# Second attention in block products: another order of VectorE's, ScalarE's and TensorE's short steps, token sums made one head earlier

## The chip, the cores and the metric

One core of a Trainium2 chip runs the whole program. The metric is the device time of one execution in microseconds (us). Everything is float32; matmuls run on a high part and a low part of each operand (three passes: high x high, high x low, low x high), so every weight block is first copied to a rounded high part by ScalarE and the rest is made by VectorE.

## The reference, cut to what matters

Two transformer-like blocks run one after the other on 512 tokens of width 2048. The change lies in the second block's chunk attention:

```python
proj = h @ w_in[l]
a_q, a_k, a_v, a_z, g_q, g_f, g_i, g_z = jnp.split(proj, offsets, axis=-1)
...
q = _rms(q, q_g); k = _rms(k, k_g)
scores = einsum(q, kb) * (dh ** -0.5)
p = softmax(where(valid, scores + bias, -inf))
out = einsum(p, vb)
att = att * jax.nn.silu(a_z)
```

It has 8 heads of width 128. Then comes a gated recurrence (`hg`, 8 heads), and the output projection.

## The kernel before

TensorE works through phases. Phase `att` has 8 heads. Heads 0 and 1 are plain: four projections (query, key, value, gate), each of 16 steps of three 512-column matmuls. Heads 2 to 7 (`att_pairs`, L1239 for TensorE, L1906 for ScalarE, L2820 for VectorE) are made from *pairs*: the query and key tiles are one pair (`keys`), the value and gate tiles another (`values`). A pair is computed with seven block products instead of eight (a Strassen-like scheme): sums and differences of weight blocks and of token blocks are multiplied and the results combined. There are 12 pairs.

Names that the change touches:

- **Product n of pair q** (`pair_product`, L1206): 8 steps of three 256-column matmuls, 24 in all, into one PSUM bank. It waits for the low part of its weight block (`block_split`) and for its bank to have been read. `hooks` maps a step number to something that is put behind that step.
- **`pair_high(q, n)`** (ScalarE, L1767) copies a weight block of 128x1024 to its high part, **`pair_low(q, n)`** (VectorE, L2659) makes the low part. `SPLIT_AT` says in which place of the order block n comes: before it is 0, 1, 2, 6, 3, 4, 5.
- **`read_pair(q, n)`** (VectorE, L2673) reads a finished bank and combines it; `first_form` and `first_corner` (ScalarE) copy two corners.
- **Token blocks**: products of pair 0 need sums of token blocks of `Y`, made in place by `t_sums(0..3)` (VectorE, L2625), rounded by `t_high` (ScalarE) and completed by `t_low` (VectorE), in heads 0 to 2.
- **The head's tail.** After the four projections of head i the rest of that head runs while the products of head i+1 do: gate (`gate_softplus`, `gate_logged`, `gate_sigmoid`, `gate_silu`), the turned value (`turn_value`, then `value_highs`, `value_lo`), the turned probabilities (TensorE `turn_head`, ScalarE `probsT_att`, VectorE `probs_lows`; two PSUM banks are used in turn, so tile j waits for `probsT` and `probs_lows` of tile j-2), `weigh_head`, and `weighed`.
- **Norm and scores of head i** run in its own `values` pair: `pair_norm` / `square_lo` / TensorE `square_sum` / `pair_rows` / `pair_normed` for query (0) and key (1), then `high` and `low` of both, `first_keys`, then four `scores` and the softmax steps `soft_in`, `exps`, `soft_out`.
- **DMA.** SyncE reloads the blocks of the next pair when a block has been split (`next_pair`); GpSimd adds further blocks onto them in an accumulating DMA (`add_block`): into `raw_block(1, 0)` and into `block_sums` (shown as `mkv` in the trace).
- **The junction to `hg`** (`first_recurrence`, L1276): 48 matmuls of 512 columns, the first 24 on the token halves that were never overwritten, then 16 that need `act_hi` restored from memory and 8 that need `act_lo` restored (GpSimd, L3285). The tail of head 7 is hooked in. SyncE reloads seven heads of `Y` (1792 KB, L759) there.

The order on each engine is written out by hand. Each engine runs its own list in order and waits on semaphores, so a step that waits holds up what is behind it on its engine.

Of the kernel before, what the change touches and what calls it, by code (L numbers as in the profile page):

```python
# [157 lines left out]
def build(nc, wt, ada, bias, far_d, xT, memT, pw, cols_d, consts_d, starts_d, masks_d, spill, y_spill, block_spill, c_row,  # L158
          cum_rows, out):
    ctx = ExitStack()  # L160
    with ctx:
# [382 lines left out]
        SPLIT_AT = (1, 2, 3, 5, 6, 7, 4)  # L544
# [61 lines left out]
        def _(sp):  # L606
# [95 lines left out]
            def next_pair(q, between=None):  # L702

                sp.wait_ge(block_split.sem, block_split.at("pair", q, SPLIT_AT[1]))
# [5 lines left out]
                sp.wait_ge(block_split.sem, block_split.at("pair", q, SPLIT_AT[6]))  # L710
                sp.dma_start(raw_block(1, 1), pair_block(q + 1, 1, 1)).then_inc(s_block[3], 16)
                sp.wait_ge(block_split.sem, block_split.at("pair", q, SPLIT_AT[3]))
                sp.dma_start(raw_block(0, 1), pair_block(q + 1, 0, 1)).then_inc(s_block[1], 16)
                sp.wait_ge(block_split.sem, block_split.at("pair", q, SPLIT_AT[4]))
                sp.dma_start(block_sums[0], pair_block(q + 1, 0, 0)).then_inc(s_third, 16)
# [35 lines left out]
            for s, n in ((1, 6), (0, 3)):  # L751
                sp.wait_ge(block_split.sem, block_split.at("pair", NPAIR - 1, SPLIT_AT[n]))
                sp.dma_start(raw[:, slot("hg", s), :], wt[TILE0["hg"] + s]).then_inc(s_raw[slot("hg", s)], 16)
# [3 lines left out]
            sp.wait_ge(product_done.sem, product_done.at("pair", NPAIR - 1, 5))  # L757
            sp.wait_ge(s_att, 16 * (NATT - 1))
            sp.dma_start(Y[:, 0:NATT - 1, :], y_spill.rearrange("k p s -> p k s")).then_inc(s_reload, 16)  # L759
            loop(sp, "hg", lambda i: [load("hg", i, j) for j in range(4)])  # L760
# [59 lines left out]
        def _(pe):  # L820
# [385 lines left out]
            def pair_product(q, n, hooks=None):  # L1206

                i, v = q // 2 + NPLAIN, q % 2
                pe.wait_ge(block_split.sem, block_split.at("pair", q, SPLIT_AT[n]))
# [29 lines left out]
            def att_pairs(i):  # L1239
# [8 lines left out]

                pair_product(keys, 0)
# [3 lines left out]
                if i > NPLAIN:  # L1253
                    turn_head(i - 1, (0, 1))
                pair_product(keys, 2)
                if i > NPLAIN:
# [3 lines left out]
                if i > NPLAIN:  # L1260
                    weigh_head(i - 1)
# [3 lines left out]
                pair_product(values, 1, {2: lambda: square_sum(1)})  # L1265
                pair_product(values, 2, {2: lambda: score(0), 6: lambda: score(1)})
# [9 lines left out]
            def first_recurrence():  # L1276
# [15 lines left out]
                hooks = {0: lambda: turn_value("att", head, 2, qkv2[:, 2, :], QT), 5: lambda: turn_head(head, (0, 1)),  # L1292
# [142 lines left out]
        def _(act):  # L1435
# [353 lines left out]
            def att(i):  # L1789
# [65 lines left out]
                gate_exp("att", i, 3, dst=2)  # L1855
                if i == NPLAIN - 1:
                    pair_high(0, 2)
# [48 lines left out]
            def att_pairs(i):  # L1906
                keys, values = pair_no(i, 0), pair_no(i, 1)
                tail = i > NPLAIN
                pair_high(keys, 6)
                if tail:  # L1910
                    gate_softplus(i - 1)
                else:
                    t_high(1)
                first_form(keys)
                if tail:
                    value_highs(i - 1)
                else:
                    t_high(3)
                pair_high(keys, 3)
                if tail:  # L1920
                    gate_sigmoid(i - 1)
                    probsT_att(i - 1, 0)
                    probsT_att(i - 1, 1)
                pair_high(keys, 4)
                if tail:
                    probsT_att(i - 1, 2)
                    probsT_att(i - 1, 3)
                first_corner(keys)
                pair_high(keys, 5)
# [7 lines left out]
                high("att", i, 0, qk2_hi, qkv2)  # L1937
                pair_rows(i, 1)
                first_form(values)
                pair_high(values, 3)  # L1940
                high("att", i, 1, qk2_hi, qkv2)
                pair_high(values, 4)
                for t in range(2):
                    exps("att", i, t, tp2[:, 0, :])
                first_corner(values)
                pair_high(values, 5)
# [148 lines left out]
        def _(dve):  # L2095
# [563 lines left out]
            def pair_low(q, n):  # L2659

                dve.wait_ge(block_hi.sem, block_hi.at("pair", q, SPLIT_AT[n]))
# [3 lines left out]
            def pair_sum(q):  # L2665
# [3 lines left out]
                if q:  # L2669
                    dve.wait_ge(block_split.sem, block_split.at("pair", q - 1, SPLIT_AT[5]))  # L2670
# [41 lines left out]
            def att(i):  # L2712
# [30 lines left out]
                else:  # L2743
                    split("att", i, 0)
                    t_sums(0)
                    t_sums(1)
                    square_lo("att", i, 0, sq2_hi[:, :], sq2_lo[:, :])
# [6 lines left out]
                else:  # L2754
                    t_sums(2)
# [18 lines left out]
                if i == NPLAIN - 1:  # L2774
                    t_sums(3)
# [3 lines left out]
                if i == NPLAIN - 1:  # L2779
                    pair_sum(0)  # L2780
                    pair_low(0, 0)
                    pair_low(0, 1)
                if i:
                    dve.wait_ge(s_att, 16 * i)
                silu_gate("att", i, 3, wk[:, 2, :])
                weighed(i)
                if i == NPLAIN - 1:
                    t_low(2)
                    pair_low(0, 2)
# [30 lines left out]
            def att_pairs(i):  # L2820
# [6 lines left out]
                pair_low(keys, 6)  # L2827
                if tail:
                    gate_logged(i - 1)
                    value_lo("att", i - 1, v2_lo, v2_hi)  # L2830
# [607 lines left out]
```

## Time and profile before

| | us |
|---|---|
| Median of 3 runs (1877.53 to 1880.18) | 1877.79 |
| The profiled execution, its own time | 1876.38 |
| Its span, first to last instruction | 1874.6 |
| TensorE busy, of the span | 1847.6 |
| VectorE busy | 1381.3 |
| ScalarE busy | 875.4 |
| GpSimd busy | 243.4 |
| Mean granted TensorE clock | 0.995 of full |

TensorE is busy 99% of the span, but its matmuls overlap in the record (a 256-column matmul is recorded as 0.28 us and the next starts 0.12 us later), so busy time hides where the issue rate halves. Waits that are recorded as idle, and distances between starts, say more. Head h of the pair stage starts at 983.73, 1034.32, 1085.90, 1137.56, 1189.15 and 1239.24 us for h = 2 to 7.

### The profile page before, as it was taken

What the parts mean: (1) busy time and instruction counts of PE and PEld (TensorE: products, weight loads), DVE (VectorE), ACT (ScalarE), POOL (GpSimd) and SP (SyncE); (2) the same over time, 40 slices, a digit from 0 to 9 for tenths busy, and PEclk for the clock granted to TensorE, in tenths of its full rate; (3) what the DMA queues carried; (4) which work ended last, traced back from release to release, by engine and by line L of the source; (5) the groups of instructions that cost most, each with busy time, mean ns of one, the idle gap of its engine ahead of it and who ended that gap; (6) DMA issues with size and microseconds to landing.
All of it is one profiled execution on the core that took longest, in us unless ns stands there. A gap on an engine that the chain in (4) does not pass through costs nothing.

```text
span 1874.6 us, 28099 instructions
## 1 busy us (share of the span) xinstructions
PE 1847.6 (99%) x10006; PEld 1590.4 (85%) x10006; DVE 1381.3 (74%) x2011; ACT 875.4 (47%) x1310; POOL 243.4 (13%) x241
## 2 busy tenths in 40 slices
PE   9999999999999999999998999999999999999999
PEld 8888888888888877887888999998888888888999
DVE  6765678888888877777777677776666666659986
ACT  6543433333333373224545555554555555556333
POOL 3500000000000003442001011000122221111121
PEclk9999999999999999999999999999999999999999
DMA  7344244554445426675337666666222222123442
GB/s 282 112 158 180 70 163 171 179 178 164 161 168 177 148 101 232 231 252 184 116 110 182 181 165 162 170 173 197 68 90 90 70 86 90 67 90 124 147 157 91
DMA packets 68620, 278.25 MB, mean 148 GB/s; under 512 B 7352, under 2 KB 12984, under 8 KB 52288
## 3 DMA queue, kind: packets, MB, share of 16 engines
q1 hardware_dynamic: 60832, 253.08, 39.0%
q0 software_dynamic: 7264, 20.97, 6.2%
q10 hardware_dynamic: 448, 3.17, 0.4%
q8 instruction: 49, 0.80, 0.2%
q14 instruction: 27, 0.22, 0.0%
HBM read 264.85 MB, written 12.35 MB: 148 GB/s over the span
## 4 chain that ended last, share of the span: by engine, by line
PE 83%; DVE 9%; ACT 4%; issue 3%; DMA 1%; DVEq 0%; POOL 0%; ACTq 0%; another core or an unknown queue 0%; POOLq 0%
PE ps_p L843 20%; PE ps_p L845 20%; PE ps_p L844 20%; DVE w_lo L2662 2%; ACT w_hi L1771 1%; PE ps_o L1008 1%; PE ps_s L1323 1%; PE ps_t L1425 1%; PE ps_p L1231 1%; PE ps_p L1232 1%; PE ps_p L1233 1%; PE ps_t L1426 1%; PE ps_t L1424 1%; PE ps_s L1425 1%; PE ps_s L1424 1%
## 5 line engine op out<-in xcount | busy, mean ns | idle before, releaser
L843 PE MATMUL ps_p<-act_hi,w_hi 128*128 128x512 f32 x1680 | 672.6, 400 | 0.3 <-DVE w_lo L2116 0.3
L845 PE MATMUL ps_p<-act_hi,w_lo 128*128 128x512 f32 x1680 | 655.9, 390 | 0.0
L844 PE MATMUL ps_p<-act_lo,w_hi 128*128 128x512 f32 x1680 | 654.6, 390 | 0.0
L845 PEld LDWEIGHTS ps_p<-act_hi,w_lo 128*128 128x128 f32 x1680 | 315.3, 188 | 68.7
L843 PEld LDWEIGHTS ps_p<-act_hi,w_hi 128*128 128x128 f32 x1680 | 315.8, 188 | 60.6 <-issue 1.2
L844 PEld LDWEIGHTS ps_p<-act_lo,w_hi 128*128 128x128 f32 x1680 | 316.2, 188 | 59.6 <-issue 0.7
L1448 ACT ACTIVATE w_hi<-raw 128x2048 fp32r<-128x2048 f32 x117 | 223.7, 1912 | 268.3 <-PE ps_p L845 251.3
L2111 DVE TENSOR_TENSOR w_lo<-raw,w_hi 128x2048 fp32r<-128x2048 f32 x115 | 263.8, 2294 | 59.5 <-ACT w_hi L1448 48.2
L2406 DVE CUSTOM_DVE_ANT_0 mkv<-mkv,c_all 128x1024 f32<-128x1024 f32 x96 | 145.7, 1554 | 3.7 <-DVE wk L2153 2.9
L3261 POOL TENSOR_TENSOR ssq_a<-ssq_a,wk 128x512 f32<-128x512 f32 x15 | 36.3, 2420 | 724.6 <-ACT wk L1712 724.6
L1232 PE MATMUL ps_p<-y_lows,w_hi 128*128 128x256 f32 x384 | 109.4, 285 | 0.0
L1608 ACT ACTIVATE tp<-tp,stat 128x128 f32<-128x128 f32 (+1 forms) x64 | 36.1, 564 | 141.7 <-DVE stat L2375 141.7
L2245 DVE SCALAR_TENSOR_TENSOR Y<-upad,cols,Y 128x512 f32<-128x512 f32 x120 | 82.1, 747 | 0.0
L3301 POOL TENSOR_TENSOR hz<-hqk,hd 128x128 f32<-128x128 f32 x48 | 34.0, 707 | 327.0 <-DVEq L2985 288.2
L1232 PEld LDWEIGHTS ps_p<-y_lows,w_hi 128*128 128x128 f32 x384 | 73.7, 192 | 0.3
L2662 DVE TENSOR_TENSOR w_lo<-mkv,w_hi 128x1024 fp32r<-128x1024 f32 x36 | 44.0, 1223 | 36.5 <-ACT w_hi L1771 36.5
L2662 DVE TENSOR_TENSOR w_lo<-raw,w_hi 128x1024 fp32r<-128x1024 f32 x48 | 58.6, 1222 | 9.3 <-ACT w_hi L1771 9.2
L1231 PE MATMUL ps_p<-act_hi,w_hi 128*128 128x256 f32 x192 | 54.8, 285 | 1.9 <-DVE qkv L2681 1.9
L2076 ACT ACTIVATE w_hi<-mkv 128x1024 fp32r<-128x1024 f32 x24 | 25.5, 1061 | 62.2 <-DVE mkv L3125 32.9
L1233 PE MATMUL ps_p<-act_hi,w_lo 128*128 128x256 f32 x192 | 54.3, 283 | 0.0
L3268 POOL DMA_DIRECT2D mkv<-wt_dram x24 | 21.0, 877 | 253.3 <-DMA mkv<-wt_dram 128.5
L1771 ACT ACTIVATE w_hi<-raw 128x1024 fp32r<-128x1024 f32 x48 | 50.3, 1050 | 6.0 <-PE ps_p L1233 6.0
(520 smaller groups left out, 3599.8 us busy)
## 6 DMA issues: line engine op xcount, KB each, us to landing
raw<-wt_dram SPq DMA_DIRECT2D x122, 1024.0 KB, 4.9
mkv<-ada_dram SPq DMA_DIRECT2D x96, 512.0 KB, 4.6
raw<-wt_dram SPq DMA_DIRECT2D x68, 512.0 KB, 5.1
mkv<-wt_dram POOLq DMA_DIRECT2D x24, 512.0 KB, 5.9
mkv<-wt_dram SPq DMA_DIRECT2D x12, 512.0 KB, 6.3
raw<-wt_dram POOLq DMA_DIRECT2D x12, 512.0 KB, 8.8
qkv<-xT_dram SPq DMA_DIRECT2D x16, 256.0 KB, 2.8
spill_dram<-Y SPq DMA_DIRECT2D x16, 256.0 KB, 2.4
```

Of the source, the lines that this page charges most:

```text
L843: mm(o, wh, hi[:, k, 0:n], start=at == 0, stop=False)
L844: mm(o, wh, lo[:, k, 0:n], start=False, stop=False)
L845: last = mm(o, wl, hi[:, k, 0:n], start=False, stop=at == KT - 1)
L1231: mm(o, wh[:, c], hi, start=n < 3 and k == 0, stop=False, skip_group_check=True)
L1232: mm(o, wh[:, c], lo, start=False, stop=False, skip_group_check=True)
L1233: last = mm(o, wl[:, c], hi, start=False, stop=k == HALF_K - 1, skip_group_check=True)
L1448: fn(w_hi[:, s, :], raw[:, s, :], ACT.Copy).then_inc(w_hi_done, 1)
L1771: fn(fast_slot(n, w_hi), PAIR_FROM[n], ACT.Copy).then_inc(block_hi.sem, 1)
L2111: tt(w_lo[:, s, :], raw[:, s, :], w_hi[:, s, :].bitcast(F32), ALU.subtract).then_inc(w_split, 1)
L2245: o.step(stt(Y[:, c, :], upad[:, c, bass.ds(tap, S)], cols[:, bass.ds(tap + (w0 + c * TAPS), 1)], Y[:, c, :], ALU.mult, ALU.add))
L2406: dve.tensor_tensor_reduce(out=w, in0=w, in1=c_all[:, n % 2 * ADA_PIECE:(n % 2 + 1) * ADA_PIECE], scale=1.0, scalar=0.0, op0=ALU.mult, op1 ...
L2662: tt(fast_slot(n, w_lo), PAIR_FROM[n], fast_slot(n, w_hi).bitcast(F32), ALU.subtract).then_inc(block_split.sem, 1)
```

## The change

- The low and high parts of a pair's weight blocks are made in the order 0 to 6; `SPLIT_AT` is gone. Block 6 moves from the fourth place to the last. SyncE's reloads follow that order, so `raw_block(1, 1)` is reloaded last and not third.
- TensorE: transposes 2 and 3 of a head's probabilities move from between products 2 and 3 into product 3 (behind its steps 1 and 4). The second square sum goes one step later, the first score from step 2 to step 4 of product 2, the second score from step 6 to behind that product.
- ScalarE and VectorE: `probs_lows` 0 and 1 are made together; the key's norm comes ahead of the query's `pair_rows`; `high` and `low` of query and key come together; blocks 3, 5 and 6 of the `values` pair take other places.
- Head 0 takes `t_sums(0)`, head 1 takes `t_sums(1)` to `(3)` a place earlier and `t_low(2)` too; in head 1's gate the steps are mixed with `pair_high(0, 2)` and `pair_low(0, 2)`.
- Junction to `hg`: the split of the first tile comes behind the fourth `soft_in`, the head-7 weighing ahead of the wait for `act_lo`, the value's transposes two steps later. The two first tiles are loaded in the other order, and the reload of `Y` waits for two more tile loads.

```diff
-        SPLIT_AT = (1, 2, 3, 5, 6, 7, 4)
 next_pair (SyncE), behind raw_block(1, 0) and raw_block(0, 0):
-                sp.wait_ge(block_split.sem, block_split.at("pair", q, SPLIT_AT[6]))
+                sp.wait_ge(block_split.sem, block_split.at("pair", q, 4))
+                sp.dma_start(raw_block(0, 1), pair_block(q + 1, 0, 1)).then_inc(s_block[1], 16)
+                sp.wait_ge(block_split.sem, block_split.at("pair", q, 5))
+                sp.dma_start(block_sums[0], pair_block(q + 1, 0, 0)).then_inc(s_third, 16)
+                sp.wait_ge(block_split.sem, block_split.at("pair", q, 7))
                 sp.dma_start(raw_block(1, 1), pair_block(q + 1, 1, 1)).then_inc(s_block[3], 16)
-                (raw_block(0, 1) behind SPLIT_AT[3], block_sums[0] behind SPLIT_AT[4])
 SyncE, junction:
-            for s, n in ((1, 6), (0, 3)):
+            for s, n in ((0, 3), (1, 6)):
+            def hg(i):
+                for j in range(4):
+                    load("hg", i, j)
+                    if isinstance(i, int) and j == 1:
+                        (the reload of Y, which stood ahead of the loop)
 TensorE, att_pairs:
                 pair_product(keys, 2)
-                if i > NPLAIN:
-                    turn_head(i - 1, (2, 3))
-                pair_product(keys, 3)
+                pair_product(keys, 3, {1: turn(2), 4: turn(3)} if tail else None)
...
-                pair_product(values, 1, {2: lambda: square_sum(1)})
-                pair_product(values, 2, {2: lambda: score(0), 6: lambda: score(1)})
+                pair_product(values, 1, {3: lambda: square_sum(1)})
+                pair_product(values, 2, {4: lambda: score(0)})
+                score(1)
 TensorE, first_recurrence:
-                hooks = {0: lambda: turn_value(...), 5: ..., 7: ...}
+                hooks = {2: lambda: turn_value(...), 5: ..., 7: ...}
...
+                weigh_head(head)
                 pe.wait_ge(s_add[1], RESTORED)
                 for k in range(HALF_K):
                     ins = step(k, lambda wh, wl, hi, lo: ((wh, lo),), last=k == HALF_K - 1)
-                    if k == 4:
-                        weigh_head(head)
 ScalarE, att_pairs:
-                pair_high(keys, 6)
...
                 pair_high(keys, 5)
-                for n in range(2):
-                    pair_high(values, n)
+                first_corner(keys)
+                pair_high(keys, 6)
+                pair_high(values, 0)
+                pair_high(values, 1)
                 pair_norm(i, 0)
                 pair_high(values, 2)
+                pair_norm(i, 1)
                 pair_rows(i, 0)
-                pair_norm(i, 1)
-                pair_high(values, 6)
+                pair_high(values, 3)
+                pair_rows(i, 1)
+                high(query), high(key), first_form(values), pair_high(values, 4), exps 0,
+                pair_high(values, 5), exps 1, first_corner(values), pair_high(values, 6), exps 2
 VectorE, att_pairs:
-                pair_low(keys, 6)
...
                 read_pair(keys, 0)
                 if tail:
                     probs_lows(i - 1, 0)
+                    probs_lows(i - 1, 1)
                 pair_low(keys, 4)
-                    probs_lows(i - 1, 1)
                 read_pair(keys, 1)
...
                 pair_low(keys, 5)
+                pair_low(keys, 6)
...
+                square_lo("att", i, 1, sq2_hi[:, :], sq2_lo[:, :])
                 pair_normed(i, 0)
-                square_lo("att", i, 1, sq2_hi[:, :], sq2_lo[:, :])
-                pair_low(values, 6)
-                low("att", i, 0, qk2_lo, qkv2, qk2_hi)
+                pair_low(values, 3)
                 pair_normed(i, 1)
                 first_keys(i)
-                pair_low(values, 3)
-                read_pair(values, 0)
+                low("att", i, 0, qk2_lo, qkv2, qk2_hi)
                 low("att", i, 1, qk2_lo, qkv2, qk2_hi)
                 o.settle()
                 dve.sem_inc(qk_ready.sem, 1)
+                read_pair(values, 0)
...
                 soft_in("att", i, 2, lambda t, e: add_bias(i, t, e))
+                pair_low(values, 6)
...
-                else:
-                    split("hg", 0, -1)
                 soft_in("att", i, 3, lambda t, e: add_bias(i, t, e))
                 bias_read(i)
+                if i == NATT - 1:
+                    split("hg", 0, -1)
 VectorE, att (heads 0 and 1): t_sums(0) goes to the end of head 0, t_sums(1), (2), (3)
 one place earlier, t_low(2) ahead of value_lo; pair_low(0, 2) between the gate's two steps.
```

## Rows read from the trace of the kernel before

**Rows 1.** Page part 1, TensorE and the others over the whole span

```profile
PE 1847.6 (99%) x10006; PEld 1590.4 (85%) x10006; DVE 1381.3 (74%) x2011; ACT 875.4 (47%) x1310; POOL 243.4 (13%) x241
```

**Rows 2.** Waits of TensorE, 960 to 1320: total us, times, longest

```profile
PE ps_t L992 <- DVE p_lo L2709: 8.2, 10, 1.5
PE ps_x L959 <- DVE sq_lo L2694: 4.0, 6, 0.7
PE ps_s L980 <- DVEq L2867: 2.8, 6, 0.5
PE ps_p L1231 <- DVE w_lo L2662: 2.0, 1, 2.0
PE ps_p L1231 <- DVE qkv L2681: 1.9, 1, 1.9
PE ps_p L1284 <- DVE qkv L2687: 1.8, 1, 1.8
PE ps_p L1284 <- DMA act_lo<-block_spill_dram: 0.5, 1, 0.5
```

**Rows 3.** Windows of heads 2, 4, 6: length, busy, granted clock, DMA share

```profile
983.73:1034.32 50.59, 45.59 (x351) 44.46 (x352) 39.98 (x56) 28.19 (x42) 5.16 (x6) 0.97 0.69 172
1085.90:1137.56 51.66, 48.88 (x379) 47.48 (x377) 36.74 (x62) 27.79 (x47) 5.18 (x6) 0.97 0.67 171
1187.40:1237.50 50.10, 47.31 (x378) 46.01 (x378) 36.75 (x63) 27.78 (x46) 5.19 (x6) 1.00 0.68 176
```

**Rows 4.** Timeline of TensorE, head 4: start, duration, line, idle before

```profile
1092.12 0.93 PE L992 MATMUL ps_t<-consts,tp 128*128 128x128 f32 x7
1092.81 0.36 PE L1231 MATMUL ps_p<-th_mid,w_hi 128*128 128x256 f32 x1
...
1098.16 0.36 PE L1231 MATMUL ps_s<-act_hi,w_hi 128*128 128x256 f32 x1
...
1102.60 0.28 PE L1231 MATMUL ps_p<-act_hi,w_hi 128*128 128x256 f32 x1
...
1105.47 0.69 PE L1008 MATMUL ps_o<-tp_r,v_hi 128*128 128x512 f32 x3
...
1107.20 0.36 PE L1231 MATMUL ps_p<-act_hi,w_hi 128*128 128x256 f32 x1
...
1116.37 0.28 PE L1231 MATMUL ps_p<-th_short,w_hi 128*128 128x256 f32 x1
...
1118.27 0.47 PE L959 MATMUL ps_x<-sq_hi,ones_r 128*128 128x512 f32 x1 [0.67 <-DVE sq_lo L2694]
```

**Rows 5.** Timelines of VectorE and ScalarE, heads 2 and 4

```profile
988.23 2.28 DVE L2657 TENSOR_TENSOR y_lows<-Y,th_mid 128x2048 fp32r<-128x2048 f32 x1
...
1095.27 0.68 DVE L2709 TENSOR_TENSOR p_lo<-ps_t,tp_r 128x512 fp32r<-128x512 f32 x1
1096.12 1.23 DVE L2662 TENSOR_TENSOR w_lo<-mkv,w_hi 128x1024 fp32r<-128x1024 f32 x1 [0.17 <-ACT w_hi L1771]
...
1114.78 0.69 ACT L1901 ACTIVATE wk<-ps_x,cols 128x512 f32<-128x512 f32 x1 [1.72 <-PE ps_x L960]
...
1116.12 0.62 ACT L1892 ACTIVATE wk<-qkv 128x512 f32<-128x512 f32 x1
```

**Rows 6.** Timeline of TensorE at the junction to hg

```profile
1290.72 0.28 PE L1233 MATMUL ps_p<-act_lo,w_lo 128*128 128x256 f32 x1
...
1309.86 0.40 PE L843 MATMUL ps_p<-act_hi,w_hi 128*128 128x512 f32 x1
...
1310.55 0.40 PE L843 MATMUL ps_p<-act_hi,w_hi 128*128 128x512 f32 x1
```

**Rows 7.** DMA issues at the junction (1285 to 1292) and at 1089.87: KB, us to landing

```profile
act_hi<-block_spill_dram POOLq DMA_DIRECT2D x1, 1024.0 KB, 6.0
act_lo<-block_spill_dram POOLq DMA_DIRECT2D x1, 1024.0 KB, 14.8
...
mkv<-wt_dram POOLq DMA_DIRECT2D x1, 512.0 KB, 7.9
```

More of the change, by code:

```diff
@@ L756, in _ @@
             load("hg", 0, -1)
[L757 to L760, printed above, removed]
+            def hg(i):
+                for j in range(4):
+                    load("hg", i, j)
+                    if isinstance(i, int) and j == 1:
+                        sp.wait_ge(product_done.sem, product_done.at("pair", NPAIR - 1, 5))
+                        sp.wait_ge(s_att, 16 * (NATT - 1))
+                        sp.dma_start(Y[:, 0:NATT - 1, :], y_spill.rearrange("k p s -> p k s")).then_inc(s_reload, 16)
+            loop(sp, "hg", hg, head=1)
             for j in range(2):
@@ L1854, in att @@
                         pair_high(0, n)
-                gate_exp("att", i, 3, dst=2)
-                if i == NPLAIN - 1:
-                    pair_high(0, 2)
+                if i < NPLAIN - 1:
+                    gate_exp("att", i, 3, dst=2)
+                    return
+                act.wait_ge(proj_done, tile_no("att", i, 3) + 2)
+                act.wait_ge(heads_done.sem, heads_done.at("att", i, 0))
+                softplus(wk[:, 2, :], ps_p[:, slot("att", 3), :]).then_inc(gate_soft.sem, 1)
+                pair_high(0, 2)
+                gate_sigmoid(i)
             def value_highs(i):
@@ L1927, in att_pairs @@
                     probsT_att(i - 1, 3)
+                pair_high(keys, 5)
                 first_corner(keys)
-                pair_high(keys, 5)
-                for n in range(2):
-                    pair_high(values, n)
+                pair_high(keys, 6)
+                pair_high(values, 0)
+                pair_high(values, 1)
                 pair_norm(i, 0)
                 pair_high(values, 2)
+                pair_norm(i, 1)
                 pair_rows(i, 0)
-                pair_norm(i, 1)
-                pair_high(values, 6)
[L1937 to L1946, printed above, removed]
+                pair_high(values, 3)
+                pair_rows(i, 1)
+                high("att", i, 0, qk2_hi, qkv2)
+                high("att", i, 1, qk2_hi, qkv2)
+                first_form(values)
+                pair_high(values, 4)
+                exps("att", i, 0, tp2[:, 0, :])
+                pair_high(values, 5)
+                exps("att", i, 1, tp2[:, 0, :])
+                first_corner(values)
+                pair_high(values, 6)
                 exps("att", i, 2, tp2[:, 0, :])
@@ L2774, in att @@
                 if i == NPLAIN - 1:
-                    t_sums(3)
+                    t_low(2)
                 value_lo("att", i, v2_lo, v2_hi)
@@ L2782, in att @@
                     pair_low(0, 1)
+                else:
+                    t_sums(0)
                 if i:
                     dve.wait_ge(s_att, 16 * i)
-                silu_gate("att", i, 3, wk[:, 2, :])
+                log_sigmoid("att", i, 3, 1, wk[:, 2, :])
+                if i == NPLAIN - 1:
+                    pair_low(0, 2)
+                do(tt(wk[:, 3, :], ps_p[:, slot("att", 3), :], wk[:, 2, :], ALU.mult))
+                dve.sem_inc(evac[slot("att", 3)], 1)
                 weighed(i)
-                if i == NPLAIN - 1:
-                    t_low(2)
-                    pair_low(0, 2)
             def bias_read(i):
@@ L2830, in att_pairs @@
                     value_lo("att", i - 1, v2_lo, v2_hi)
+                else:
+                    t_low(1)
                 pair_low(keys, 3)
-                if not tail:
-                    t_low(1)
                 read_pair(keys, 0)
@@ L2836, in att_pairs @@
                     probs_lows(i - 1, 0)
+                    probs_lows(i - 1, 1)
                 pair_low(keys, 4)
-                if not tail:
-                    t_low(3)
-                if tail:
-                    probs_lows(i - 1, 1)
                 read_pair(keys, 1)
```

43 lines of the change are left out of this document (22 added, 21 removed).

## The prediction

> **What bounds the kernel now.** I read the page's first part, then TensorE's waits, then windows over single heads, then the timeline of TensorE across one head, and last the timelines of the two engines that feed it. TensorE is busy 99% of the span [rows 1], so nothing outside its own path can matter much, and nothing that only shortens VectorE or ScalarE. But the busy share hides two things. The waits of the pair stage and of the junction add up to 8.2 + 4.0 + 2.8 + 2.0 + 1.9 + 1.8 + 0.5 = 21.2 us [rows 2]: nearly all of TensorE's idle time in the whole kernel (1874.6 - 1847.6 = 27) stands in the 330 us that the diff touches. And the windows show something that is in no wait: head 4 takes 51.66 at a granted clock of 0.97, head 6 takes 50.10 at 1.00, with the same work [rows 3]. Five of the six heads (2, 3, 4, 5 and 7) have it.
>
> The timeline says where. A product is 24 matmuls and takes 1105.47 - 1102.60 = 2.87 at the full clock [rows 4]. Seven transposes take 1092.81 - 1092.12 = 0.69, so 0.1 each, and the weighing of a head 1107.20 - 1105.47 = 1.73 [rows 4]. Product 2 of `keys` and the three transposes behind it start at 1092.81 and product 3 at 1098.16: 5.35 where 2.87 + 0.3 = 3.17 is work, so 2.18 lost. Product 3 then takes 1102.60 - 1098.16 = 4.44 instead of 2.87: 1.57 lost, because after that gap the granted clock fell to its lower level (1.2 instead of 2.4 GHz) for a stretch. The difference of the heads' windows, 51.66 - 50.10 = 1.56, is that same 1.57 [rows 3]: the gap stood in head 6 as well and the clock didn't fall there. After the shorter waits (0.7 and 0.5) no fall shows.
>
> **The change part by part.**
>
> *Transposes 2 and 3.* What they wait for is a chain: the tail's softplus, the value, the sigmoid and `probsT` 0 on ScalarE, then `probs_lows` 0 on VectorE, 1095.27 to 1095.95; then `pair_low(keys, 4)`, which itself waits 0.17, 1096.12 to 1097.35; then `probs_lows` 1, which the last transpose needs [rows 5]. Nothing in the diff makes the first link earlier: the block-6 pieces that go away ran in time in which VectorE waited for the softplus and ScalarE for a read bank. So `probs_lows` 0 is ready at 1095.95 as now, plus about 0.15 to reach TensorE. TensorE asks for it later: product 3 can start at 1092.81 + 2.87 = 1095.7, two steps (6 matmuls of 0.12) end at 1096.4. That is 0.3 of slack where 2.18 were lost. `probs_lows` 1 now follows at once: done by 1095.95 + 0.68 = 1096.6 at most, and asked for after three more steps and transpose 2, at 1096.4 + 0.2 + 1.08 = 1097.7: 1.0 of slack. Behind them, `pair_low(keys, 4)` ends near 1097.8 and is asked for by product 4 at 1095.7 + 2.87 + 0.3 = 1098.9. So the whole loss goes: 2.18 for each of heads 3 to 7 and 1.57 for four of them, 10.9 + 6.3 = 17.2. The bounds: if transpose 2 were 0.5 late each time and the clock fell as now, 2.5 + 6.3 would stay, and 8 be gained; nothing can be gained beyond 17.2.
>
> *Second square sum.* From 1116.37 to 1118.27 stand nine matmuls (1.08): 0.82 lost a head [rows 4]. ScalarE ran `pair_rows(0)` from 1114.78 ahead of the key's norm at 1116.12, 1.34 [rows 5]. Now the norm is first, so its low part comes 1.3 earlier, and TensorE asks 0.36 later. 0.82 x 6 = 4.9 gained. The price is that `pair_rows(0)` comes 1.3 later, and with it the first score, which has moved by two steps (0.7) and whose path loses `pair_low(values, 6)` (1.22, a piece as in [rows 5]); I count that as slack of about 0.5.
>
> *Second score.* 2.8 in six heads [rows 2], with a restart of 0.1 each 0.55 a head. Its path loses `pair_low(values, 6)` and `read_pair(values, 0)`, 1.6 together, and it is asked for after the product instead of one step before its end. 3.3 gained.
>
> *Head 2 (first pairs).* TensorE waits 2.0 for block 2's low part and 1.9 for `read_pair(0, 1)` [rows 2], and the clock is 0.97 over the 50.59 [rows 3], so another 1.5 as in head 4. In front of both stands `t_low(2)`, 2.28 at 988.23 [rows 5], between the weighing of head 1 and `pair_low(0, 2)`. It now runs in head 1 where `t_sums(3)` ran, and `t_sums(0)` runs at the end of head 0, where VectorE waits for the gate's softplus anyway. `pair_low(0, 2)` comes out of the gate's own waits at about 987.5, and product 2 asks at 983.73 + 2 x 2.9 = 989.6. `t_low(1)` then ends at 991.1 and block 3 at 992.3, which product 3 wants at 992.5: the tightest spot, 0.1. `t_low(3)` and block 5 end at 997.9 before 998.3. Gain 2.0 + 1.9 + 1.5 = 5.4, between 3 and 6.
>
> *The block-6 pieces* are moved into idle stretches of both engines (VectorE is busy 37 of 51.7 [rows 3]) with nothing waiting behind them but the softmax steps. *The reloads*: block (1, 1) is issued some 10 us later in the pair and needed last. What is needed earlier than before is the accumulated `block_sums[1]`: `pair_high(keys, 5)` used to wait for a free slot until late and will now start right behind `probsT` 3, about 12.3 after the head's start. Its DMA is issued 1089.87 - 1085.90 = 4.0 after the start and lands 7.9 later [rows 7], at 11.9. So 0.4 of slack on ScalarE, and 2.8 more until product 5 asks. I cost it at nothing.
>
> *Junction.* From the end of the last product (1290.72 + 0.12) to the next projection (1309.86) are 19.0 [rows 6]. Work in it: 48 matmuls of (1310.55 - 1309.86) / 3 = 0.23, so 11.0, and 1.73 for weighing and 14 transposes of 0.1: 14.2 [rows 4, 6]. The loss of 4.8 is the 1.8 wait for `read_pair(values, 3)`, the 0.5 wait for the restored `act_lo` [rows 2], and a stretch at the lower clock. With block 5 earlier in the last pair VectorE reaches the split of the first `hg` tile and then `read_pair(values, 3)` before the last product ends; the wait goes, and the low clock after it. TensorE then arrives some 4 us sooner at `act_lo`, which landed only at 1291.31 + 14.8 = 1306.1 [rows 7]. That DMA ran beside 1792 KB of `Y`; its twin of the same size and form took 6.0 alone. With `Y` behind two more tile loads I take 8 (between 6.0 and 14.8, nearer to the undisturbed row), so 1299.4, and the weighing now stands ahead of that wait: no wait. If it kept its 14.8, TensorE would be held to 1306.1 + 8 x 0.23 = 1307.9, and 1.9 would be the whole gain of the junction. Against the gain: `hg`'s second tile is now loaded as its block 6 is split, 6.5 before the last product's end, beside the restore of `act_hi`, and the last tail's chain starts behind its split. I take 4.0 gained, between 0 and 4.8.
>
> On such transfers the Trainium skill (DMA: Bandwidth & Descriptors, "Issuing engines are not separate DMA queues") has a rule that speaks against this part: DMAs started by sync, scalar or gpsimd interleave on the same 16 engines. By that rule the second tile and `act_hi`, issued by two engines at one time, slow each other, and the last tail starts later; the sum would then be some 2 us worse. The same rule is what makes moving `Y` worth something. The trace agrees, with 14.8 against 6.0 for one form [rows 7].
>
> **Sum.** 17.2 + 4.9 + 3.3 + 5.4 + 4.0 = 34.8. Each tight spot has 0.1 to 0.5 of slack worked out from rows that agree within 0.1, so a few tenths will stay here and there; I take off 1.5. Against the profiled execution: 1876.4 - 33.3 = 1843.1. The median of the runs lies 1.4 above it: 1877.8 - 33.3 = 1844.5. I say 1844.
>
> **The rivals.**
>
> *A: the short waits stay in part.* The 0.3 at transpose 2 and the 0.5 at the first score may be negative by as much. Each then costs its lateness, and if the clock falls, 1.57 a head as now. For: the softplus chain is untouched by the change. Against: gaps of 0.7 and 0.5 did not bring the clock down in any of six heads. Price: about 10 to 14 back, of which 6.3 clock: 1855 to 1858.
>
> *B: the junction gives nothing* (`act_lo` as late as now or the last tail late behind the tile). 4.0 back: 1848. It lies in the forecast's own range.
>
> *C: slower, by the accumulating DMA.* `pair_high(keys, 5)` now stands on ScalarE ahead of the corner, block 6, both first blocks of `values` and the norm, so a late `block_sums[1]` holds them all. It has 0.4 + 2.8 of slack and 5.2 of gain a head to eat: the change turns slower from a landing of 7.9 + 3.2 + 5.2 = 16.3 on. The row shows 7.9, and even twice the size beside `Y` took 14.8 [rows 7]. At 18 it costs 10 us more than now: 1887.
>
> *D: nothing*: the waits are put down to the wrong releaser and others stand right behind each. For: three engines run in near lockstep here. Against: the chain above leaves slack at every one. About 1876.
>
> **How the numbers follow.** Forecast (with B in it, 1839 to 1850) 0.74; A 0.16; something between A and D 0.05; D 0.02; C 0.03. The range 1838 to 1857 holds the forecast and most of A. A measurement of this kernel can tell about 0.2% (3.8 us) from no change. Faster by more: 0.95; within: 0.02; slower: 0.03.
>
> **What would show it.** After: heads 3 to 7 of about 46.5 us each with granted clock 1.00, head 2 of about 44 to 45; no wait of L992 over 0.3; L959 and L980 waits near zero; the wait for `read_pair(0, 1)` and block 2 gone; junction of 14.5 to 16; `act_lo` landing in under 10. Heads at 48 or more with a clock of 0.97 mean A. A wait of ScalarE's L1771 for `mkv`'s DMA means C. The plain heads and `hg`, `out2` and `fast` should keep their lengths; if `hg` head 0 grows, the later reload of `Y` is in the way of its tiles, which I have taken to have 20 us of room.

## The result and the profile after

| | us |
|---|---|
| Median before, in the runs beside those of after | 1877.71 (1877.53 to 1880.18) |
| Median after, 4 runs | 1844.88 (1843.74 to 1845.87) |
| Ratio, 95% interval | 0.9822 (0.9805 to 0.9839) |
| Profiled execution after, its own time / its span | 1844.08 / 1842.2 |

The profiled execution is 32.3 us shorter (1876.38 - 1844.08); predicted were 33.3. The places it came from, by the starts of the heads in both timelines (head 2 starts at 983.46 after):

| | before | after | gained | predicted |
|---|---|---|---|---|
| head 2 | 50.59 | 47.91 | 2.7 | 6.8 (5.4, and 0.82 + 0.55) |
| heads 3 to 7 | 256.5 | 231.1 | 25.4 | 24.05 (17.2, and 5 x 1.37) |
| junction | 19.0 | 14.96 | 4.1 | 4.0 |

The page's first part, which answers [rows 1]:

```profile
PE 1833.5 (100%) x10006; PEld 1582.1 (86%) x10006; DVE 1380.2 (75%) x2011; ACT 875.7 (48%) x1310; POOL 243.5 (13%) x241
```

VectorE and ScalarE do as much as before; only TensorE's record shrank, by 14 us, less than half of the gain. The waits of TensorE from 960 to 1320 (total us, times, longest) answer [rows 2]:

```profile
PE ps_t L1235 <- DVE w_lo L2673: 2.3, 1, 2.3
PE ps_s L1235 <- DVE w_lo L2673: 0.3, 1, 0.3
PE ps_x L963 <- DVE sq_lo L2705: 0.2, 1, 0.2
PE ps_t L996 <- DVE p_lo L2720: 0.2, 1, 0.2
```

Of 21.2 us 3.0 are left, and the largest, 2.3, is a wait that was not there before. The windows of heads 2, 4 and 6 and of the junction (length, busy, granted clock, DMA share, GB/s) answer [rows 3]:

```profile
983.46:1031.37 47.91, 45.18 (x352) 44.08 (x352) 37.50 (x55) 28.49 (x42) 5.16 (x6) 0.96 0.72 182
1077.59:1123.84 46.25, 46.25 (x378) 45.81 (x377) 36.57 (x62) 27.78 (x47) 5.18 (x6) 1.00 0.77 192
1170.05:1216.30 46.25, 46.25 (x378) 45.81 (x377) 36.56 (x62) 27.77 (x47) 5.18 (x6) 1.00 0.77 191
1262.51:1277.47 14.96, 14.74 (x75) 12.00 (x74) 8.29 (x13) 6.47 (x11) 0.89 (x1) 1.00 0.90 250
```

Heads 4 and 6 have no idle time and the full clock, and are now equally long; before, they differed by 1.56. (The window that [rows 3] gives for head 6 begins 1.75 before the head; by its own starts, 1189.15 to 1239.24, the head takes 50.09, so the reading stands.) TensorE's timeline of head 4 (start, duration, line) answers [rows 4]: the first row of product 3, its two hooked transposes, and the later places of the second square sum and of the scores:

```profile
1087.38 0.28 PE L1235 MATMUL ps_s<-act_hi,w_hi 128*128 128x256 f32 x1
...
1088.11 0.38 PE L996 MATMUL ps_t<-consts,tp 128*128 128x128 f32 x2
...
1089.40 0.27 PE L996 MATMUL ps_t<-consts,tp 128*128 128x128 f32 x1
...
1105.80 0.39 PE L963 MATMUL ps_x<-sq_hi,ones_r 128*128 128x512 f32 x1
...
1109.47 0.38 PE L979 MATMUL ps_s<-tp,qkv 128*128 128x128 f32 x2
1110.76 0.28 PE L984 MATMUL ps_s<-qk_hi 128*128 128x256 f32 x1
```

None has an idle note. Head 2 is the exception. Its timelines on SyncE, GpSimd, ScalarE, VectorE and TensorE, in the order of the chain:

```profile
989.20 0.33 SPq L695 DMA_DIRECT2D y_spill_dram<-wk  x1
989.63 0.42 SPq L705 DMA_DIRECT2D raw<-wt_dram  x1
...
997.49 0.86 POOL L3281 DMA_DIRECT2D raw<-wt_dram  x1 [8.60 <-DMA raw<-wt_dram]
...
1004.13 1.06 ACT L1777 ACTIVATE w_hi<-raw 128x1024 fp32r<-128x1024 f32 x1 [4.57 <-DMA raw<-wt_dram]
...
1004.19 1.23 DVE L2682 TENSOR_TENSOR mkv<-raw 128x1024 f32<-128x1024 f32 x1 [5.08 <-issue]
1005.33 1.22 DVE L2673 TENSOR_TENSOR w_lo<-raw,w_hi 128x1024 fp32r<-128x1024 f32 x1
...
1006.61 0.57 PE L1235 MATMUL ps_t<-act_hi,w_hi 128*128 128x256 f32 x1 [2.27 <-DVE w_lo L2673]
1006.97 0.42 PE L1236 MATMUL ps_t<-act_lo,w_hi 128*128 128x256 f32 x1
```

SyncE's store of head 1 (L695) stands ahead of the load of `raw_block(1, 0)` (L705) and waits for the weighing. The load is issued at 989.63 and lands 7.6 later; GpSimd adds onto it (lands 6.6 later, at 1004.1); only then can ScalarE round it and VectorE make `pair_sum(values)` and the low part. Matmuls behind the wait start 0.21 apart and not 0.12: the granted clock from 1006.60 to 1009.10 is 0.51. Before, the same chain was ready about as late: its load, issued behind the store at 988.77, landed 4.6 later, and GpSimd's addition landed 9.8 after its issue, at 1003.5 (GpSimd's row in the timeline, and the row of the DMA issues with KB and us to landing):

```profile
993.68 0.86 POOL L3268 DMA_DIRECT2D raw<-wt_dram  x1 [0.88 <-DMA raw<-wt_dram]
```

```profile
raw<-wt_dram POOLq DMA_DIRECT2D x1, 512.0 KB, 9.8
```

But TensorE, held up by its two earlier waits, came only at 1009.8.

### The profile page after: what moved, and what is told of

It reads as the page before. It is cut to its first block, busy times and chain, and to the rows that moved or that the text cites. A ratio compares the mean times of both kernels' runs of the same rounds, so it can differ in the third digit from the quotient of the medians.

```text
span 1842.2 us, 28086 instructions
## 1 busy us (share of the span) xinstructions
PE 1833.5 (100%) x10006; PEld 1582.1 (86%) x10006; DVE 1380.2 (75%) x2011; ACT 875.7 (48%) x1310; POOL 243.5 (13%) x241
## 4 chain that ended last, share of the span: by engine, by line
PE 93%; DVE 5%; issue 1%; ACT 1%; DMA 0%; DVEq 0%; SPq 0%; another core or an unknown queue 0%; ACTq 0%
PE ps_p L847 20%; PE ps_p L849 20%; PE ps_p L848 20%; PE ps_p L1236 3%; PE ps_p L1237 3%; PE ps_p L1235 3%; PE ps_o L1012 1%; PE ps_s L1329 1%; PE ps_t L1431 1%; PE ps_t L1432 1%; PE ps_t L1430 1%; PE ps_t L996 1%; PE ps_s L1431 1%; PE ps_s L1430 1%; PE ps_s L1432 1%
## 5 line engine op out<-in xcount | busy, mean ns | idle before, releaser
L3274 POOL TENSOR_TENSOR ssq_a<-ssq_a,wk 128x512 f32<-128x512 f32 x15 | 36.3, 2420 | 724.7 <-ACT wk L1718 724.7
```

## The experiments

Twelve kernels. *Period* is the distance from one weighing to the next, mean over heads 3 to 6 (the kernel after: 46.23; the kernel before: 51.23, mean of head starts 1034.32 to 1239.24). The medians of before beside them were 1876.6 to 1877.7. The runs were spread over four chips, but all profiles start this stage together (the weighing ahead of head 2 stands between 981.30 and 981.76).

**e1_turns_back**, on the kernel after:

```diff
-                pair_product(keys, 3, {1: turn(2), 4: turn(3)} if tail else None)
+                if tail:
+                    turn_head(i - 1, (2, 3))
+                pair_product(keys, 3)
```

> The changed kernel with one part undone: TensorE makes transposes 2 and 3 of the head before between products 2 and 3 again, in heads 3 to 7; VectorE and ScalarE keep their new order. Theory 1 (the loss follows the size of the wait): VectorE now rounds the two probability blocks one after the other right behind product 2's eviction, so TensorE waits about 1 us a head where it waited 2.18, and stays at full clock: 5 heads x 1 = 5 us, 1850. Rival (any stop at this place halves the clock behind it): the 1.57 us of half clock comes with it in each head: 5 x 2.6 = 13 us, 1858. Rival A of the prediction (the order on VectorE was the cause, the place on TensorE is idle talk): nothing, 1845.

Measured 1847.63 (1846.28 to 1848.71). Period 46.50: 0.27 a head, 1.35 in all, and no wait is recorded at these transposes; they take 0.51 between the products. The rest stands in head 2, which this edit does not touch: there this profiled run has a wait of 3.74 where after has 2.27, a second one of 1.11 at the square sum where after has 0.20, and a stretch at the lower clock (matmuls 0.21 apart from 1011.4 to 1015.9). By its median the run lies midway between theory 1 and the third reading; by the period the third is nearest: with VectorE's new order the place on TensorE hardly matters.

**e2_hooks_only**, on the kernel before:

```diff
-                if i > NPLAIN:
-                    turn_head(i - 1, (2, 3))
-                pair_product(keys, 3)
+                pair_product(keys, 3, {1: lambda: turn_head(i - 1, (2,)), 4: lambda: turn_head(i - 1, (3,))}
+                             if i > NPLAIN else None)
```

> The kernel before with one part of the change alone: TensorE makes transposes 2 and 3 inside product 3 (after its second and fifth step) in heads 3 to 7; VectorE and ScalarE keep the old order. Theory: product 3's matmuls cover the evictions that the transposes waited for, so nearly all of 17.2 us goes: 1877.8 - 15 to 17 = 1861 to 1863. Rival (the hooks come too early for VectorE's old order, which rounds probability block 3 only behind the next low block): the wait moves into product 3, at most half goes: 1868 or more.

Measured 1863.95 (1862.56 to 1864.64), 13.7 below before. Period 48.28, 2.95 below before, with the granted clock at 1.00 from 1051.8 to 1245. Waits of TensorE, 960 to 1320:

```profile
PE ps_x L959 <- DVE sq_lo L2693: 4.0, 6, 0.7
PE ps_p L1283 <- DMA act_lo<-block_spill_dram: 3.0, 1, 3.0
PE ps_s L980 <- DVEq L2866: 3.0, 6, 0.6
```

The ten waits at the transposes are gone, with VectorE's old order; the heads gain what the theory says. Heads 3 to 7 take 241.3, 15.2 less than before. Two places gave some of it back: the wait for `act_lo` grew from 0.5 to 3.0, which made the junction 20.1 long, 1.1 more than before, and head 2 took 1.4 more, where the clock fell twice and not once. So in heads 3 to 7 the same edit is worth 15 where it is the first and 1.4 where it is the last.

**e3_norm_back**, on the kernel after: `pair_rows(0)` ahead of the key's norm on ScalarE, `pair_normed(0)` ahead of the second square on VectorE.

```diff
-                pair_norm(i, 1)
                 pair_rows(i, 0)
+                pair_norm(i, 1)
```

> The changed kernel with the order of the second attention's norm step undone: VectorE normalises pair 0 ahead of the second square, ScalarE makes its rows ahead of the second norm. Theory (the term of the prediction holds): TensorE's second square sum waits 0.8 us again and the second score 0.55 us again in some or all heads: 1.37 x 6 = 8 us if both return, 4.9 if only the first, so 1850 to 1853. Rival (the waits had been produced by the late start of the step, which the other parts have also changed): 1845 to 1846.

Measured 1848.81 (1847.34 to 1849.99). Period 46.77: 0.54 a head, of which 0.31 is recorded as a wait (L963), and the score does not wait. The wait in head 2 was 3.65 in this run. In between the two theories: about 3.2 for six heads, not 4.9; the rest of the 3.9 between the medians goes with the longer wait in head 2.

**e5_store_later**, on the kernel after, in head 2 only:

```diff
-                    if i == NPLAIN:
-                        store_head(i - 1)
-                    next_pair(pair_no(i, 0))
+                    next_pair(pair_no(i, 0), between=(lambda: store_head(i - 1)) if i == NPLAIN else None)
```

> The changed kernel with one edit more: in head 2, SyncE issues the two raw block loads of its first pair ahead of the store of head 1, not behind it. The store waits for the weighing at 989.17 us of the profiled run, so the loads wait with it and are issued at 989.63; ahead of it they could go at about 984.6. Theory (the wait of 2.27 us ahead of the first values product of head 2 comes from this chain: load 7.6 us, POOL's accumulating transfer 6.6 us, ScalarE's high part, VectorE's pair sum): the wait goes, and with it the half clock behind it; head 2 falls from 47.9 to some 44 to 45 us and the kernel to 1841. Rival (the keys product's evictions, or VectorE's own queue, are as late anyway): the wait goes down by under 0.5 us, the time stays at 1844.5 or more.

Measured 1839.56 (1839.53 to 1839.66), 5.3 below after, ratio to before 0.9795 (0.9782 to 0.9809). SyncE, GpSimd and ScalarE in head 2:

```profile
984.45 0.33 SPq L705 DMA_DIRECT2D raw<-wt_dram  x1
...
988.84 0.86 POOL L3279 DMA_DIRECT2D raw<-wt_dram  x1
...
998.55 1.06 ACT L1775 ACTIVATE w_hi<-raw 128x1024 fp32r<-128x1024 f32 x1 [0.66 <-PE ps_p L1235]
```

The load goes 5.2 earlier and the wait is gone; the weighings of heads 1 and 2 are 61.41 apart, 65.79 after: 4.4 gained, so head 2 takes 43.5, 7.1 below before where 6.8 were predicted. The chain is shown, by the trace and by the medians, though the intervals of the two ratios to before just touch (0.9809 here, 0.9805 for after). This is also the fastest kernel of the study. Its five runs lie within 0.13 us, those of after within 2.1: so most of that spread came with this chain. All further runs start from this kernel, as differences of 0.3 us can be seen on it.

**f1_lows_back**:

```diff
 VectorE:
                     probs_lows(i - 1, 0)
-                    probs_lows(i - 1, 1)
                 pair_low(keys, 4)
+                if tail:
+                    probs_lows(i - 1, 1)
```

> Base of this and the next runs: the changed kernel with the two raw loads ahead of the store (1839.6 us, five runs within 0.13). Here one part is undone: VectorE rounds probability block 3 (the second probs_lows) behind pair_low(keys, 4) again; TensorE's two transposes stay inside product 3. Theory (two edits that each cover the same wait: the product in front hides what VectorE is late by): TensorE loses some 0.3 us a head, as it lost 0.27 a head when only the transposes went back: 1841. Rival (VectorE's order carries the gain, TensorE's place only the rest): 1.5 us or more a head, 1847.

Measured 1839.70 (1839.55 to 1839.81), period 46.23: nothing. **f2_both_back** has this edit and that of e1:

> The same base with both parts undone: VectorE's old place for probability block 3 and TensorE's old place for transposes 2 and 3. Theory (either alone would do, so the gain of 17.2 us in the prediction belongs to both together): the loss is far above the sum of the two single ones (0.3 + 0.3 a head): 2.2 of wait a head, 11 us, and 1.6 more in the heads where the granted clock falls behind it: 1851 to 1857. Rival (the rest of VectorE's new order has already moved these blocks): the sum of the two, 1842 to 1843.

Measured 1848.14 (1847.98 to 1848.20), 8.6 slower; period 47.94. Waits of TensorE:

```profile
PE ps_t L994 <- DVE p_lo L2720: 7.1, 5, 1.4
```

Undone alone the two cost 0 (f1) and 0.27 a head (e1, on the kernel after), together 1.71. Each covers the wait that the other would leave; this is shown. The clock did not fall. Five heads lost 8.6, so with both undone half of the 17.2 is still unaccounted for.

**f3_pool_late**:

```diff
-                pool.wait_ge(block_split.sem, block_split.at("pair", q, 3))
+                pool.wait_ge(block_split.sem, block_split.at("pair", q, 4))
                 add_block(block_sums[1], q, 0, 1, 2)
```

> The same base with POOL's accumulating transfer into block_sums[1] issued one block split later (behind block 4, not 3), 5.2 us later by the profiled run. Rival C of the prediction gave this transfer's path a slack of 0.4 + 2.8 us. Theory: ScalarE's high part of block 5 comes 4.5 us later, less 2.8, so TensorE stands before product 5 for 1.7 us in each head: 6 x 1.7 = 10 us, and up to 1.5 a head more for the clock: 1850 to 1859. Rival (with an idle queue the transfer lands sooner, or the slack is larger): under 3 us, at most 1842.5.

Measured 1875.89 (1873.58 to 1879.17): 36.3 us slower, nearly all that was gained. Waits of TensorE, and ScalarE's and TensorE's rows in head 4:

```profile
PE ps_p L1233 <- DVE w_lo L2671: 15.7, 8, 6.0
PE ps_x L864 <- DVEq L2824: 8.6, 5, 1.7
```

```profile
1108.27 1.06 ACT L1775 ACTIVATE w_hi<-mkv 128x1024 fp32r<-128x1024 f32 x1 [5.01 <-DMA mkv<-wt_dram]
...
1110.71 0.39 PE L1233 MATMUL ps_p<-act_hi,w_hi 128*128 128x256 f32 x1 [2.01 <-DVE w_lo L2671]
...
1131.48 1.06 ACT L1775 ACTIVATE w_hi<-mkv 128x1024 fp32r<-128x1024 f32 x1 [3.55 <-DMA mkv<-wt_dram]
```

Product 5 of `keys` is late by 2.0, near the 1.7 worked out from rival C's slack; but GpSimd's issue came 11.3 after the start of head 4 (1100.26 - 1088.99), 7.8 later than in the kernel after and not 5.2, so that agreement is partly luck. The `values` pair has the same transfer, and there ScalarE waits 3.55 in front of the softmax steps, and the turned value of the next head (L864) is late by 1.7. With the first pair's 6.0 in head 2 and 5.0 a head elsewhere the price is 36 where the theory had 10 to 19.

**f4_y_early**: `Y` reloaded ahead of the loop over the `hg` tiles.

> The same base with the reload of Y in its old place, ahead of the loads of the hg tiles. Theory of the prediction (Y's 1792 KB made act_lo land after 14.8 us, and moving them behind the second hg tile removed TensorE's wait for it): act_lo lands after 14 us or more, TensorE waits for it again, 1.5 to 2.2 us: 1841 to 1842. Rival (act_lo's landing depends on other traffic at that place, or the new order of TensorE leaves room enough): under 0.5 us, 1839.5 to 1840.

Measured 1844.96 (1844.81 to 1845.13), 5.4 slower. TensorE's wait, and the DMA issues from 1240 to 1320 (KB, us to landing), first of this kernel, then of the kernel after, which answer [rows 7]:

```profile
PE ps_p L1284 <- DMA act_lo<-block_spill_dram: 3.6, 1, 3.6
```

```profile
Y<-y_spill_dram SPq DMA_DIRECT2D x1, 1792.0 KB, 14.8
act_hi<-block_spill_dram POOLq DMA_DIRECT2D x1, 1024.0 KB, 8.6
act_lo<-block_spill_dram POOLq DMA_DIRECT2D x1, 1024.0 KB, 16.4
```

```profile
Y<-y_spill_dram SPq DMA_DIRECT2D x1, 1792.0 KB, 9.7
act_hi<-block_spill_dram POOLq DMA_DIRECT2D x1, 1024.0 KB, 8.4
act_lo<-block_spill_dram POOLq DMA_DIRECT2D x1, 1024.0 KB, 7.6
```

The theory is right and its price too low: 3.6 of wait, and 1.5 more because the eight matmuls behind it then take 3.33 (clock 0.55) and not 8 x 0.23.

**f5_tokens_back**: `t_low(2)` and `pair_low(0, 2)` behind the weighing of head 1 again.

```diff
(both steps are taken out of their new places further up)
                 weighed(i)
+                if i == NPLAIN - 1:
+                    t_low(2)
+                    pair_low(0, 2)
```

> The same base (1839.6) with one part of the head 2 edits undone: VectorE makes t_low(2) and pair_low(0, 2) behind the weighing of head 1 again. Theory (the head 2 term of the prediction was right in itself and was only covered up by the late raw load): TensorE waits for pair_low(0, 2) again, about 2.0, perhaps 1.9 more for the evictions behind it, and up to 1.5 for the clock: 1842 to 1845. Rival (with the loads early, VectorE catches up within the three products): under 1 us, 1840.

Measured 1842.34 (1841.91 to 1842.76), 2.8 slower, with one wait of 2.0 for block 2, none for the evictions and no fall of the clock: at the low end of the theory. So with all the rest new these two steps carry 2.8 of the 5.4 that the prediction gave to head 2; the moves of `t_sums` were not undone in any run.

**f6_three_back** is f2 with the edit of e3; **f7_pe_back** is f6 with TensorE's old places of the second square sum and of the scores:

```diff
-                pair_product(values, 1, {3: lambda: square_sum(1)})
-                pair_product(values, 2, {4: lambda: score(0)})
-                score(1)
+                pair_product(values, 1, {2: lambda: square_sum(1)})
+                pair_product(values, 2, {2: lambda: score(0), 6: lambda: score(1)})
```

> The same base with three parts undone in the second attention: TensorE's place of transposes 2 and 3, VectorE's place of probability block 3, and the order of the second norm on ScalarE and VectorE. The first two together lost 1.7 a head (a wait of 1.43, no fall of the clock), though the kernel before had a wait of the same size (0.20 + 1.46) and the clock fell behind it in four of five heads. Theory (the falling clock hangs on the sum of stops in a head, so it comes back when the second square sum stops too): 1.7 + 0.55 of waits and 1.57 of clock a head, 1839.6 + 16 to 19 = 1856 to 1859. Rival (the parts only add): 1848.1 + 3 = 1851.

> As the run before, and TensorE also asks for the second square sum, the first score and the second score in its old places. What is then left of the change in the second attention is the place of the block 6 pieces and the reloads that follow from it. Theory (the second score's recorded wait of 0.46 understates it: matmuls queued ahead of it are slow too, and the timeline of the kernel before shows 0.83 lost there): 0.8 a head for the second square sum, 0.8 for the scores: 1.0 to 1.3 a head more than the run before. Rival (the score was late only through pair_low(values, 6), which stays moved): the square sum alone, under 0.4 a head more.

Measured 1851.39 (1851.32 to 1851.49) and 1852.00 (1851.97 to 1852.30); periods 48.46 and 48.53. Both theories fall and their rivals hold: the norm adds its 0.52 a head and no more, the clock stays at full, and TensorE's old places add 0.1. Waits of TensorE in f7:

```profile
PE ps_t L994 <- DVE p_lo L2719: 5.2, 5, 1.1
PE ps_x L961 <- DVE sq_lo L2704: 4.0, 6, 0.7
```

No wait at a score. Between f7 and the kernel before 2.7 of the 5.0 a head are left, and with them what made the score late. The expectations of f7 and g1 give all of that to block 6, and this is wrong: more of the change is still in f7. In heads 3 to 7 VectorE's `read_pair(values, 0)` still stands behind the low parts of query and key, no longer ahead of the scores; `pair_low(values, 3)` and ScalarE's `high` and `first_form` keep their new places too. VectorE's rows in head 5 of before, and of f7, from the last read of the pair before to the gate's step behind the softplus, tell more:

```profile
1141.14 0.42 DVE L2689 TENSOR_TENSOR wk<-ps_p,wk 128x256 f32<-128x256 f32 x1
...
1143.68 0.69 DVE L2802 SCALAR_TENSOR_TENSOR wk<-wk 128x512 f32<-128x512 f32 x1 [0.39 <-ACT wk L1465]
```

```profile
1127.79 0.42 DVE L2699 TENSOR_TENSOR wk<-ps_p,wk 128x256 f32<-128x256 f32 x1
...
1130.32 0.69 DVE L2815 SCALAR_TENSOR_TENSOR wk<-wk 128x512 f32<-128x512 f32 x1 [1.53 <-ACT wk L1470]
```

It is 2.54 with `pair_low(keys, 6)` in between and 2.53 without: that piece ran in time in which VectorE waited anyway, as the prediction said. This points to the steps around the score in `values`, where no run separates block 6 from `read_pair(values, 0)`. **g1_block6_back** undoes block 6 alone, on the base: `SPLIT_AT` and the old order of the reloads, and

```diff
+                pair_low(keys, 6)
                 if tail:
                     gate_logged(i - 1)
...
+                pair_low(values, 6)
                 pair_low(values, 3)
```

> The same base (1839.6) with only the place of block 6 undone: both engines make its high and low part first among the later blocks of keys, and ahead of block 3 of values, and the reloads follow their old order; TensorE's places, the probability blocks, the norm's order, head 2's token sums and Y stay new. With everything else of heads 3 to 7 undone (the run before) a head takes 48.5 us, the kernel before takes 50.09 in the head without the fall of the clock and 51.6 in the others, so 1.6 to 3.1 a head hang on block 6 there, against the prediction's nothing. Theory (block 6 matters only behind a late softplus chain and a late score, and the new places on TensorE cover it, as they covered the probability blocks): 0 to 0.5 a head, 1840 to 1843. Rival (VectorE's and ScalarE's time in front of the score is lost whatever TensorE does): 0.8 to 1.6 a head in six heads, 1844 to 1850, more if the clock falls.

Measured 1843.78 (1843.62 to 1843.86), 4.2 slower, ratio to before 0.9815 (0.9797 to 0.9832). Waits of TensorE:

```profile
PE ps_s L978 <- DVE tp L2714: 1.5, 6, 0.3
PE ps_s L1234 <- DVE w_lo L2672: 1.4, 1, 1.4
```

Period 46.74, 0.51 a head, now at the first score, and 1.6 in head 2. So with all the rest new the place of block 6 costs more than nothing, and less than the rival's 0.8 to 1.6 a head.

## Why the prediction was right, and where not

**The total** (1844, measured 1844.9) holds, and by the mechanism: the gain stands where TensorE's recorded and unrecorded losses stood, and the other engines' work is unchanged. That it holds within 1 us is in part luck: head 2 missed its term by 4.1, while heads 3 to 7 gave 1.4 more than theirs and the 1.5 taken off for small losses was not needed there.

**Transposes 2 and 3** (17.2). In the kernel after nothing of this loss is left, as predicted, and "0.3 of slack" at transpose 2 was enough in every head. But the term names one edit and the runs show several that overlap: undone alone the move costs 1.4, with the probability block 8.6, added alone to the kernel before it gives 15 in heads 3 to 7. Such a term is right as the price of a wait, not as the price of an edit.

**Second square sum and second score** (4.9 and 3.3). The norm's order is worth 0.52 to 0.54 a head on the kernels in which it was undone; the 0.82 is what was lost at this place in the kernel before, and no run changed the order alone there. The score term was too small: TensorE's recorded wait at L980 is 0.46, but in head 6 before it took from 1222.27 to 1226.54 for what now takes from 1107.68 to 1111.12, so 4.27 - 3.44 = 0.83 and not 0.55. Over heads 3 to 7 this gives the 1.4 by which they beat the prediction.

**Head 2** (5.4, and 1.4 of the terms above) is the step that failed: 2.7 came. The tightest spot was not product 3, which waited 0.3; it was product 0 of the `values` pair, whose DMA chain I had not followed back to SyncE's queue. The step checked VectorE's list against TensorE's only up to block 5 of `keys`, and did not ask when the block that `pair_sum(values)` reads would land. e5 gives the missing 4.4 back with one edit on SyncE.

**Block 6** was costed at nothing. For the whole change that was the safe side; as an attribution it was wrong. Its move is worth 0.5 a head, and 4.2 in all, with all the rest new (g1). From f7's period to that of before there are 2.7 more (51.23 - 48.53), 1.2 of it the clock (1.57 in three of the four heads); what part of that is block 6, and what part `read_pair(values, 0)` and the other steps still new in f7, stays open. The prediction had named both for the second score.

**Junction** (4.0, measured 4.1). f4 shows the mechanism: the order of `Y` makes `act_lo` land after 7.6 to 8.0 or after 16.4. Had it stayed, the junction would not have kept "1.9" but lost more than it gained (5.4 against 4.1), since the clock falls behind that wait; rival B was priced too mildly. By the Trainium skill (DMA: Bandwidth & Descriptors, "Issuing engines are not separate DMA queues") transfers of several issuers share the 16 engines. The trace agrees: `act_hi` beside the second tile's load took 8.4 where it took 6.0. Nothing waited for it, and the 2 us that the prediction set against the junction by that rule did not come.

**Rival A** did not come. **Rival C** did not either: `block_sums[1]`, issued 3.5 after the start of head 4, landed after 8.1 and ScalarE took it without a wait. But f3 shows how near it was: issued 7.8 later in head 4, it costs more than this change gains. I had the slack in `keys` about right and left out the same transfer in `values`.

## What to carry to other kernels

When waits are removed from the bound engine, it arrives earlier at everything: follow each of its next inputs back through every queue to the DMA's issue, and look there for an unrelated instruction that waits ahead of it. An edit's worth depends on which others are in; undo edits in pairs before you credit one. A spread of 2 us between runs of one kernel that shrinks to 0.1 with one load moved was itself a sign that this load stood on the path.

## What was not expected of the hardware

The granted clock does not follow the length of the stop in these runs. It fell behind a wait of 2.27 (after, head 2) and of 3.62 (f4), and in before behind 1.97 in head 2, behind 0.20 + 1.46 in four of five heads and behind 1.84 at the junction. It did not fall behind five waits of 1.43 in f2, behind 1.98 in f5, nor behind 3.03 in e2; in e1 the matmuls behind 3.74 still start 0.12 apart, and it fell only behind the 1.11 that followed. Windows behind the stops of after, f4, e2 and f5 (clock is the third number from the end):

```profile
1006.60:1009.10 2.50, 2.29 (x10) 2.03 (x10) 2.11 (x3) 2.15 (x3) 0.00 (x0) 0.51 0.42 62
```

```profile
1274.90:1278.30 3.40, 3.37 (x9) 2.70 (x10) 0.00 (x0) 0.00 (x0) 0.00 (x0) 0.55 0.00 0
```

```profile
1286.00:1300.00 14.00, 10.94 (x52) 8.77 (x52) 3.33 (x7) 3.18 (x6) 0.00 (x0) 1.00 0.45 150
```

```profile
991.60:996.00 4.40, 4.18 (x33) 3.97 (x34) 4.40 (x4) 0.77 (x1) 1.75 (x2) 1.00 0.63 108
```

In f3 two stops at one place, product 5 of `keys`, differ by 0.04: 1.97 in head 3, where the clock fell, and 2.01 in head 4, where it did not.

```profile
1058.40:1061.00 2.60, 2.51 (x11) 2.52 (x12) 2.60 (x4) 1.92 (x2) 0.73 (x1) 0.52 0.18 44
1110.60:1113.00 2.40, 2.29 (x19) 2.29 (x20) 2.34 (x4) 1.75 (x2) 0.43 (x1) 1.00 0.19 27
```

By the Trainium skill (TensorE: Matmul & The Clock Gate, "What's actually happening") the window over which activity is judged runs freely and isn't started by the kernel; a stop may then fall well or badly in it. These rows don't contradict that, and no run here tests it. Why the clock fell in the kernel before stays open; in heads 3 to 7 it is 6.3 of the 32 us. With what part of the change that ended can't be said either: e2's edit alone ended it there, and undoing that edit with others (f2, f6, f7) did not bring it back.
